# First output stage of a two-layer decoder kernel: the next layer's transposed input is made by VectorE and short-run transfers instead of TensorE

## The chip, the core and the metric

The kernel runs on one core of one Trainium2 chip. The metric is the device time of one execution in microseconds; the time of a kernel is the median of its runs. TensorE is called PE here, VectorE DVE, ScalarE ACT, GpSimd POOL, SyncE SP. "SPq" is SP's queue of transfer issues.

## What is computed

The reference is one inference step of a two-layer decoder trunk on 2048 prompt tokens and 64 sample tokens, width 1024. Each layer projects x, runs two parallel head groups (windowed attention and a gated linear recurrence), and ends in the part that matters here:

```python
mix = jnp.einsum('btc,cd->btd', jnp.concatenate([attn, o_hg], axis=-1), w_out)
h = _layernorm(DN_ALPHA * x + mix, ln_g, ln_b)
gate = jax.nn.sigmoid(jnp.einsum('btd,de->bte', h, w_pg))
y = h + gate * jnp.einsum('btp,pd->btd', p, w_pp)
```

y is the output of the layer and the x of the next one. All is float32; each product is made as three PE products of "high" and "low" parts of its operands.

## The kernel before

The tokens are 17 tiles of 128 (NT = 17; tile 16 holds the samples). Each layer is three stages one after another: attention, recurrence, output. Each stage runs over all 17 tiles. `output_phase` (L1873) is called for layer 0 and for layer 1; `more` is true in layer 0 only, and all that the change touches stands under `more`.

For tile n the output stage does this. PE makes `mix` (L2158), 24 matmuls for each half of 512 columns, into MX. DVE adds the residual row (`add_row`, L2075), normalises (`norm`, L2084), POOL applies gain and bias (`affine`, L1970): the result h lies in `hb[k]`, two buffers by turns. PE transposes h in eight blocks of 128 by 128 into the PSUM tile HT (`turn_h`, L2167). ACT copies HT to `hh` (`high_h`, L2012), DVE makes the remainder `hl` (`low_h`, L2096). PE makes `gate` (L2179, 48 matmuls) out of hh and hl and then `ple` (L2187, 12 matmuls). ACT takes the tanh (L2020); DVE blends and adds into `hb[k]` (`embed`, L2103, two instructions): this is y, and the semaphore `y_done` counts it. SP stores it to `y_all` (`store_y`, L1904).

The next layer reads x with the width on the partitions, from the DRAM tensor `xT1[n]`, shape [128, 8, 128]: partition p, chunk c, token t hold y[t, 128c + p]. Before the change PE makes this: `turn_y(n)` (L2195) transposes the eight blocks of y into HT, once `h_low` shows that DVE has read the h that lay there; ACT copies HT to the SBUF tile `yT` (`copy_yT`, L2022); SP stores `yT` (`store_yT`, L1908), one transfer with 4 KB for each partition.

Each engine has its list of instructions in a fixed order, with semaphores between the engines. The orders around the change:

- PE, step n: mix(n+1) half 0, turn_h(n), mix(n+1) half 1, turn_y(n-1), gate(n), ple(n).
- DVE, step n: low_h(n), add_row(n+1), norm(n+1), embed(n).
- ACT, step n: high_h(n), split_m(n+2), copy_yT(n-1), gate_tanh(n), split_p(n+1).
- SP, step n: load_row(n+2), load_p(n+2), store_y(n), load_m(n+3), store_yT(n-1).

For tile 16 there is no mix left to make. PE runs turn_h(16), turn_y(15), gate(16), ple(16), turn_y(16). SP issues in this stretch store_y(15), store_yT(14), four loads of the next layer's weights (L197), store_yT(15). The y of tile 16 is taken by the next layer directly out of HT.

There is one `yT` tile. Before, ACT waits in copy_yT(n) until the store of tile n-1 has landed (`yT_st`).

Of the kernel before, what the change touches and what calls it, by code (L numbers as in the profile page):

```python
# [25 lines left out]
P = 128  # L26
DEPTH = 2
D = 1024
KC = D // P
# [3 lines left out]
NT = SEQ // P + 1  # L33
# [92 lines left out]
def counted(value, names):  # L126
# [22 lines left out]
    **counted(NT, "m_high m_split mix_ps p_high p_split h_sum stats_done var_done ve_done rstd_done centred scaled h_done hT_ps"),  # L149
    **counted(NT, "h_high h_low gate_ps tanh_done ple_ps blend y_done"),  # L150
    **counted(16 * NT, "m_in row_in p_in"), "ln_in": 32, "y_st0": 16 * (PAIRS + 1), "y_st1": 16 * PAIRS,
    **counted(2 * KC + PC, "w_high w_split"), **counted(NT, "yT_ps yT_sb"), "yT_st": 16 * NT}


class Weights:
# [216 lines left out]
def attention_phase(nc, block, layer, C, dram, S, weights, following, lead, given, prior):  # L372
# [7 lines left out]
    with ExitStack() as ctx:  # L380
# [312 lines left out]
        def _(dve):  # L693
# [110 lines left out]
            if layer == 0:  # L804
                given.prepare(dve)
            else:
                dve.wait_ge(*prior["y_st0"].at(16 * (PAIRS + 1)))
                dve.wait_ge(*prior["y_st1"].at(16 * PAIRS))
                dve.wait_ge(*prior["yT_st"].at(16 * NT))
            dve.tensor_scalar(nsink[:, :], C["sinks"][:, layer, :], -1.0, None, ALU.mult).then_inc(S["sink_done"].sem, 1)  # L810
            dve.wait_ge(*S["sink_done"].at(1))

# [1060 lines left out]
def output_phase(nc, block, layer, C, dram, S, weights, lead, first_part, prior):  # L1873
# [3 lines left out]
    with ExitStack() as ctx:  # L1877
# [12 lines left out]
        @block.sync  # L1890
        def _(sp):
            def load_m(n):
                wait(sp, S["m_split"], n)
                sp.dma_start(mraw[:, :, :], dram["mixT"][tile_of(n)]).then_inc(S["m_in"].sem, 16)

            def load_row(n):
                wait(sp, S["h_sum"], n)
                sp.dma_start(xrow[:, :], dram["x_rows" if layer == 0 else "y_all"][n]).then_inc(S["row_in"].sem, 16)

            def load_p(n):  # L1900
                wait(sp, S["p_split"], n)
                sp.dma_start(praw[:, :, :], dram["pT"][layer, n]).then_inc(S["p_in"].sem, 16)

            def store_y(n, k):  # L1904
                sp.wait_ge(*S["y_done"].at(n + 1))
                sp.dma_start(dram["y_all"][n], hb[k][:, :]).then_inc(stored[k].sem, 16)

            def store_yT(n):  # L1908
                if not more:
                    return  # L1910
                sp.wait_ge(*S["yT_sb"].at(n + 1))
                sp.dma_start(dram["xT1"][n], yT[:, :, :]).then_inc(S["yT_st"].sem, 16)

            load_row(1)
            load_p(1)

            def step(n, k):
                load_row(n + 2)
                load_p(n + 2)
                store_y(n, k)  # L1920
                load_m(n + 3)
                if not (isinstance(n, int) and n == 0):
                    store_yT(n - 1)

            step(0, 0)
            with sp.Fori(1, PAIRS) as j:
                step(2 * j - 1, 1)
                load_row(2 * j + 2)
                load_p(2 * j + 2)
                store_y(2 * j, 0)  # L1930
                with sp.If(j < PAIRS - 1):
                    load_m(2 * j + 3)
                store_yT(2 * j - 1)
            if more:
                sp.wait_ge(*S["mix_ps"].at(NT))
                lead.load(sp, 0, 4)
            store_y(NT - 2, 1)
            store_yT(NT - 3)
            if more:
                lead.load(sp, 4, KC)  # L1940
            store_yT(NT - 2)
            store_y(NT - 1, 0)
            store_yT(NT - 1)
            sp.wait_ge(*S["y_st0"].at(16 * (PAIRS + 1)))
            sp.wait_ge(*S["y_st1"].at(16 * PAIRS))
            if more:
                sp.wait_ge(*S["yT_st"].at(16 * NT))

        @block.gpsimd
        def _(pool):  # L1950
# [49 lines left out]
        @block.scalar  # L2000
        def _(act):
            def split_m(n, k):
                act.wait_ge(*S["m_in"].at(16 * n + 16))
                wait(act, S["mix_ps"], n - 1)
                act.activation(mh[k][:, :, :], mraw[:, :, :], ACT.Copy).then_inc(S["m_high"].sem, 1)

            def split_p(n):
                act.wait_ge(*S["p_in"].at(16 * n + 16))
                wait(act, S["ple_ps"], n)
                act.activation(ph[:, :, :], praw[:, :, :], ACT.Copy).then_inc(S["p_high"].sem, 1)  # L2010

            def high_h(n):  # L2012
                act.wait_ge(*S["hT_ps"].at(n + 1))
                wait(act, S["gate_ps"], n)
                act.activation(hh[:, :, :], HT[:, :], ACT.Copy).then_inc(S["h_high"].sem, 1)

            def gate_tanh(n):
                act.wait_ge(*S["gate_ps"].at(n + 1))
                wait(act, S["y_done"], n)
                act.activation(th[:, :], GT[:, :], ACT.Tanh, scale=0.5).then_inc(S["tanh_done"].sem, 1)  # L2020

            def copy_yT(n):  # L2022
                if not more:
                    return
                act.wait_ge(*S["yT_ps"].at(n + 1))
                wait(act, S["yT_st"], 16 * n)
                act.activation(yT[:, :, :], HT[:, :], ACT.Copy).then_inc(S["yT_sb"].sem, 1)

            split_m(2, 0)
            for c in range(KC, KC + 6):  # L2030
                weights.round(act, S, layer, c)
            high_h(0)
            for c in range(KC + 6, weights.chunks):
                weights.round(act, S, layer, c)

            def step(n, split=None):
                high_h(n)
                if split is not None:
                    split_m(*split)
                if not (isinstance(n, int) and n == 0):  # L2040
                    copy_yT(n - 1)
                gate_tanh(n)
                split_p(n + 1)

            gate_tanh(0)
            split_p(1)
            step(1, (3, 1))
            with act.Fori(1, PAIRS) as j:
                step(2 * j, (2 * j + 2, 0))
                high_h(2 * j + 1)  # L2050
                with act.If(j < PAIRS - 1):
                    split_m(2 * j + 3, 1)
                copy_yT(2 * j)
                gate_tanh(2 * j + 1)
                split_p(2 * j + 2)
            high_h(NT - 1)
            if more:
                act.wait_ge(*S["mix_ps"].at(NT))
                lead.round(act, 0, 4)
            copy_yT(NT - 2)  # L2060
            gate_tanh(NT - 1)
            if more:
                act.wait_ge(*S["ple_ps"].at(NT))
                lead.round(act, 4, 5)
                act.wait_ge(*S["yT_ps"].at(NT))
                lead.split_high(act, HT)
                lead.round(act, 5, 6)
                act.wait_ge(*lead.S["x_split"].at(1))
            copy_yT(NT - 1)
            if more:  # L2070
                lead.round(act, 6, KC)

        @block.vector
        def _(dve):
            def add_row(n, k, mixed=MX):  # L2075
                dve.wait_ge(*S["mix_ps"].at(n + 1))
                dve.wait_ge(*S["row_in"].at(16 * n + 16))
                if more:
                    wait(dve, S["yT_ps"], n - 1)
                wait(dve, stored[k], 16 * (n // 2) if isinstance(n, int) else 8 * (n - k))  # L2080
                dve.scalar_tensor_tensor(out=hb[k][:, :], in0=xrow[:, :], scalar=ALPHA, in1=mixed[:, :],
                                         op0=ALU.mult, op1=ALU.add).then_inc(S["h_sum"].sem, 1)
# [20 lines left out]
            def embed(n, k):  # L2103
# [6 lines left out]
                dve.scalar_tensor_tensor(out=hb[k][:, :], in0=th[:, :], scalar=0.5, in1=hb[k][:, :],  # L2110
                                         op0=ALU.mult, op1=ALU.add).then_inc(S["y_done"].sem, 1)

            add_row(0, 0)
            norm(0, 0)
            add_row(1, 1, HT)
# [6 lines left out]
            def step(n, k):  # L2122
                low_h(n)
                add_row(n + 1, 1 - k)
                norm(n + 1, 1 - k)
                embed(n, k)

            norm(1, 1)
            embed(0, 0)
            step(1, 1)  # L2130
            with dve.Fori(1, PAIRS) as j:
                step(2 * j, 0)
# [11 lines left out]
        def _(pe):  # L2144
# [21 lines left out]

            def turn_h(n, k):  # L2167
                pe.wait_ge(*S["h_done"].at(n + 1))
                if more:
                    wait(pe, S["yT_sb"], n - 1)  # L2170
                else:
                    wait(pe, S["h_low"], n)
                if isinstance(n, int) and n == 0:
                    pe.wait_ge(*S["h_sum"].at(2))
                for c in range(KC):
# [19 lines left out]
            def turn_y(n, k):  # L2195
                if not more:
                    return
                pe.wait_ge(*S["y_done"].at(n + 1))
                pe.wait_ge(*S["h_low"].at(n + 2)) if not (isinstance(n, int) and n == NT - 1) else wait(pe, S["yT_sb"], n)
                for c in range(KC):  # L2200
                    t = pe.transpose(HT[:, c * P:(c + 1) * P], hb[k][:, c * P:(c + 1) * P], C["ident"][:, :])
                t.then_inc(S["yT_ps"].sem, 1)
# [2 lines left out]
            def step(n, k, mixes=True):  # L2205
# [2 lines left out]
                turn_h(n, k)  # L2208
                if mixes:
                    mix(n + 1, 1, 1 - k)  # L2210
                if not (isinstance(n, int) and n == 0):
                    turn_y(n - 1, 1 - k)
                gate(n)
                ple(n)

# [16 lines left out]
                step(2 * j + 1, 1)  # L2232
            n = NT - 1
            turn_h(n, 0)
            turn_y(n - 1, 1)
            gate(n)
            ple(n)
            turn_y(n, 0)
# [225 lines left out]
```

## Time and profile before

| | us |
|---|---|
| median of 3 runs | 2735.33 |
| lowest and highest | 2734.08, 2740.19 |
| the profiled execution, its own time | 2740.13 |
| its span, first to last instruction | 2738.3 |
| PE busy | 2644.4 (97% of the span) |
| DVE busy | 1514.6 (55%) |
| ACT busy | 1048.6 (38%) |
| POOL busy | 1038.6 (38%) |

The profiled execution took 4.80 us more than the median. The output stage of layer 0 lies at about 936 to 1381 us of the span. Times in the rows further on are from the start of the span. A row of the timeline has start, duration, engine, line, operation, written tile, read tiles, and in brackets the idle time before it with what ended it. Matmuls overlap, so that one lasts longer than the distance to the next.

### The profile page before, as it was taken

Reading aid. Unit: us, or ns where it says so; the run is one execution under the profiler, and the core shown is the slowest. Engines: PE = TensorE matmul, PEld = TensorE weight load, DVE = VectorE, ACT = ScalarE, POOL = GpSimd, SP = SyncE. Lnnn points to the kernel's source line nnn. Section 1 sums busy time; section 2 is a strip of 40 time slices with the busy share of each in tenths; the row PEclk is TensorE's granted clock in tenths of the full one; section 3 lists DMA queues with packets and bytes.
Section 4 is the critical chain, followed back from the end, with each engine's and each line's share of the span. In section 5 each row is a group of like instructions: output and inputs, shape, how many; then the busy total and the mean of one; then the engine's idle time right before and its main releaser. Section 6 shows DMA issues by size and latency. Waiting matters only on the chain.

```text
span 2738.3 us, 54412 instructions
## 1 busy us (share of the span) xinstructions
PE 2644.4 (97%) x21010; PEld 2158.7 (79%) x21010; DVE 1514.6 (55%) x3052; ACT 1048.6 (38%) x2305; POOL 1038.6 (38%) x959
## 2 busy tenths in 40 slices
PE   7999989999999799999989999899999997999998
PEld 6777768888888678888777777688888886788887
DVE  5566675777767822222345656657777767322322
ACT  3333354555555511111233333545555555111111
POOL 2222214555555433333212222145555564333232
PEclk9999999999999899999999999989999998999999
DMA  4111141011111522222421111410111005211220
GB/s 169 47 34 46 35 160 47 29 51 40 36 32 38 193 83 77 94 90 73 146 102 47 35 46 36 159 44 33 42 49 36 32 31 200 68 67 66 68 73 33
DMA packets 103450, 190.75 MB, mean 70 GB/s; under 512 B 11744, under 2 KB 64992, under 8 KB 101216
## 3 DMA queue, kind: packets, MB, share of 16 engines
q1 hardware_dynamic: 102864, 188.49, 20.7%
q8 instruction: 112, 1.84, 0.3%
q14 instruction: 42, 0.34, 0.0%
q10 hardware_dynamic: 432, 0.08, 0.0%
HBM read 138.53 MB, written 51.90 MB: 70 GB/s over the span
## 4 chain that ended last, share of the span: by engine, by line
PE 90%; DVE 3%; ACT 2%; issue 2%; DMA 1%; POOL 1%; SPq 1%; DVEq 0%; POOLq 0%; ACTq 0%
PE r_Z L121 25%; PE a_Z L121 16%; PE o_GT L2152 13%; PE o_MX L2152 12%; PE o_PL L2152 3%; PE a_T L977 2%; PE r_LV L1714 2%; PE a_SC L956 2%; PE o_HT L2176 1%; PE r_M L1746 1%; PE r_O L1741 1%; PE r_O L1740 1%; PE a_SC L966 1%; PE r_Z L259 1%; PE r_LV L1710 1%
## 5 line engine op out<-in xcount | busy, mean ns | idle before, releaser
L121 PE MATMUL r_Z<-w_rec_high,w_rec_xh 128*128 128x512 f32 x1024 | 423.4, 414 | 1.5 <-DVE r_kT L1488 0.9
L121 PE MATMUL r_Z<-w_rec_high,w_rec_xl 128*128 128x512 f32 x1024 | 403.7, 394 | 0.0
L121 PE MATMUL r_Z<-w_rec_low,w_rec_xh 128*128 128x512 f32 x1024 | 402.8, 393 | 0.0
L121 PE MATMUL a_Z<-w_attn_high,w_attn_xh 128*128 128x512 f32 (+1 forms) x816 | 304.4, 373 | 15.4 <-DVE w_attn_low L213 13.1
L121 PE MATMUL a_Z<-w_attn_high,w_attn_xl 128*128 128x512 f32 (+1 forms) x816 | 291.7, 357 | 0.0
L121 PE MATMUL a_Z<-w_attn_low,w_attn_xh 128*128 128x512 f32 (+1 forms) x816 | 291.7, 357 | 0.0
L1266 POOL TENSOR_TENSOR r_qE<-r_qT,r_E 128x256 f32<-128x256 f32 x230 | 186.9, 813 | 261.5 <-ACT r_E L1370 150.8
L1370 ACT ACTIVATE r_E<-r_E 128x512 f32<-128x512 f32 x230 | 145.2, 632 | 311.5 <-DVE r_E L1525 309.3
L121 PEld LDWEIGHTS r_Z<-w_rec_high,w_rec_xl 128*128 128x128 f32 x1024 | 193.8, 189 | 42.7
L121 PEld LDWEIGHTS r_Z<-w_rec_high,w_rec_xh 128*128 128x128 f32 x1024 | 193.9, 189 | 41.2 <-issue 2.9
L121 PEld LDWEIGHTS r_Z<-w_rec_low,w_rec_xh 128*128 128x128 f32 x1024 | 194.5, 190 | 34.5
L2152 PE MATMUL o_GT<-w_out_high,o_hh 128*128 128x512 f32 x512 | 203.4, 397 | 5.9 <-issue 5.9
L2107 DVE SCALAR_TENSOR_TENSOR o_th<-o_th,o_PL 128x1024 f32<-128x1024 f32 x34 | 41.5, 1222 | 297.8 <-PE o_PL L2152 297.8
L2152 PE MATMUL o_MX<-w_out_high,o_mh 128*128 128x512 f32 x480 | 191.3, 399 | 11.3 <-POOL o_ml L1954 11.3
L2152 PE MATMUL o_GT<-w_out_low,o_hh 128*128 128x512 f32 x512 | 201.4, 393 | 0.0
L2152 PE MATMUL o_GT<-w_out_high,o_hl 128*128 128x512 f32 x512 | 201.3, 393 | 0.0
L1266 POOL TENSOR_TENSOR r_kE<-r_kT,r_E 128x256 f32<-128x256 f32 x230 | 198.2, 862 | 0.0
L121 PEld LDWEIGHTS a_Z<-w_attn_high,w_attn_xh 128*128 128x128 f32 x816 | 155.7, 191 | 43.7 <-issue 21.4
L2152 PE MATMUL o_MX<-w_out_low,o_mh 128*128 128x512 f32 x480 | 188.4, 392 | 0.0
L2152 PE MATMUL o_MX<-w_out_high,o_ml 128*128 128x512 f32 x480 | 188.3, 392 | 0.0
L2020 ACT ACTIVATE o_th<-o_GT 128x1024 f32<-128x1024 f32 x34 | 35.0, 1029 | 396.9 <-PE o_GT L2152 376.4
L121 PEld LDWEIGHTS a_Z<-w_attn_high,w_attn_xl 128*128 128x128 f32 x816 | 155.6, 191 | 23.9
(290 smaller groups left out, 5633.1 us busy)
## 6 DMA issues: line engine op xcount, KB each, us to landing
dram_y_all<-o_hb SPq DMA_DIRECT2D x34, 512.0 KB, 2.9
w_attn_xraw<-dram_xT SPq DMA_DIRECT2D x33, 512.0 KB, 3.6
w_rec_whole<-dram_w_in SPq DMA_DIRECT2D x16, 1024.0 KB, 13.2
o_mraw<-dram_mixT SPq DMA_DIRECT2D x32, 512.0 KB, 4.3
r_xraw<-dram_xT SPq DMA_DIRECT2D x30, 512.0 KB, 3.6
w_attn_whole<-dram_w_in SPq DMA_DIRECT2D x16, 640.0 KB, 7.7
dram_mixT<-a_mixT SPq DMA_DIRECT2D x136, 64.0 KB, 2.1
dram_mixT<-r_u SPq DMA_DIRECT2D x34, 256.0 KB, 2.2
```

The source lines that it names most:

```text
L121: mm = pe.matmul(out, a[:, c, :], b[:, c, :], start=(first and c == chunks[0] and a is xh and b is wh), stop=(last and c == chunks[-1] and ...
L259: pe.matmul(self.banks[what], x[:, c, :], w.high[:, c, self.columns[what]], start=(c == 0 and x is self.xh[0]), stop=False)
L956: mm = pe.matmul(scores[r:r + 64, 4 * s + i, r:r + 192], qT[rows, i, r:r + 64], keys[:, first_key + r:first_key + r + 192], start=True, st ...
L966: t = pe.transpose(turned[:, h, :], probs[:, h, :], C["ident"][:, :])
L977: mm = pe.matmul(T[d, :], v[tile][:, d], pT[:, i, 4 * s:4 * s + 4, :].rearrange("p h t -> p (h t)"), start=(i == 0), stop=(i == 1))
L1266: op = pool.tensor_tensor(to, halves(flat(q_or_k), h)[half], halves(E[i][:, :], h)[half], ALU.mult)
L1370: act.activation(E[l % 2][:, :], E[l % 2][:, :], ACT.Exp).then_inc(S["level_exp"].sem, 1)
L1710: mm = pe.matmul(to[r:r + NEAR, g * h:g * h + h], kE[i][:, g * P + r:g * P + r + NEAR], qE[i][:, g, q], start=True, stop=True)
L1714: mm = pe.matmul(to[r:r + NEAR, g * 16:g * 16 + 16], kE[i][:, g * P + r:g * P + r + NEAR], qE[i][:, g, r // 2:r // 2 + 16], start=True, st ...
L2020: act.activation(th[:, :], GT[:, :], ACT.Tanh, scale=0.5).then_inc(S["tanh_done"].sem, 1)
L2107: dve.scalar_tensor_tensor(out=th[:, :], in0=th[:, :], scalar=1.0, in1=PL[:, :], op0=ALU.add, op1=ALU.mult).then_inc(S["blend"].sem, 1)
L2152: mm = pe.matmul(out[0][:, out[1]], a[:, c, :], w, start=(c == 0 and a is high and b is wh), stop=(c == chunks - 1 and a is low))
```

## The change

In layer 0, for tiles 0 to 15, PE no longer transposes y and ACT no longer copies it. DVE does it instead: `turn_y(n, k)` stands in DVE's list right behind `embed(n, k)` and turns y within blocks of 32 by 32, straight into `yT`. A block stays at its place, so the four blocks of 32 partitions have to be moved: `store_yT` is now four transfers, one for each group of 32 partitions of `yT`, whose destination is taken apart so that each run is 32 tokens, 128 bytes. `turn_y` waits until the four stores of the tile before have landed. Tile 16 still goes over PE, ACT and one transfer. PE's and DVE's waits on `yT_ps` and `yT_sb` that guarded HT and `hb` are relaxed. The place of `store_yT(n-1)` in SP's list is the same. The core of the diff:

```diff
@@ output_phase, sync engine
                 sp.wait_ge(*S["yT_sb"].at(n + 1))
-                sp.dma_start(dram["xT1"][n], yT[:, :, :]).then_inc(S["yT_st"].sem, 16)
+                if isinstance(n, int) and n == NT - 1:
+                    sp.dma_start(dram["xT1"][n], yT[:, :, :]).then_inc(S["yT_st"].sem, 16)
+                    return
+                to = dram["xT1"][n].rearrange("(q r) c t -> r c q t", q=4)
+                for i in range(0, P, 32):
+                    sp.dma_start(to[:, :, :, i:i + 32], yT[i:i + 32, :, :].rearrange("r c (q t) -> r c q t", q=4))\
+                        .then_inc(S["yT_st"].sem, 16)
@@ scalar engine
             def copy_yT(n):
-                act.wait_ge(*S["yT_ps"].at(n + 1))
-                wait(act, S["yT_st"], 16 * n)
+                act.wait_ge(*S["yT_ps"].at(1))
+                act.wait_ge(*S["yT_st"].at(64 * n))
@@ step, and the same in the loop and for the last tiles
-                if not (isinstance(n, int) and n == 0):
-                    copy_yT(n - 1)
                 gate_tanh(n)
@@ vector engine
                 if more:
-                    wait(dve, S["yT_ps"], n - 1)
+                    wait(dve, S["yT_sb"], n - 1)
...
+            def turn_y(n, k):
+                if not more:
+                    return
+                dve.wait_ge(*S["y_done"].at(n + 1))
+                wait(dve, S["yT_st"], 64 * n)
+                dve.transpose(yT[:, :, :].rearrange("p c t -> p (c t)"), hb[k][:, :]).then_inc(S["yT_sb"].sem, 1)
...
                 embed(n, k)
+                turn_y(n, k)
@@ tensor engine
             def turn_h(n, k):
-                if more:
-                    wait(pe, S["yT_sb"], n - 1)
-                else:
-                    wait(pe, S["h_low"], n)
+                wait(pe, S["h_low"], n)
...
                 if mixes:
                     mix(n + 1, 1, 1 - k)
-                if not (isinstance(n, int) and n == 0):
-                    turn_y(n - 1, 1 - k)
                 gate(n)
                 ple(n)
...
             turn_h(n, 0)
-            turn_y(n - 1, 1)
             gate(n)
```

## Rows read from the trace of the kernel before

**Rows 1.** The page: chain that ended last, shares by engine and by line

```profile
PE 90%; DVE 3%; ACT 2%; issue 2%; DMA 1%; POOL 1%; SPq 1%; DVEq 0%; POOLq 0%; ACTq 0%
```

**Rows 2.** Chain that ended last, 1150 to 1300 us: start, us, work

```profile
1222.77 5.44 PE o_MX L2152 x24
1228.22 0.87 PE o_HT L2176 x8
1229.09 5.46 PE o_MX L2152 x24
1234.55 0.87 PE o_HT L2201 x8
1235.42 10.90 PE o_GT L2152 x48
1246.32 2.72 PE o_PL L2152 x12
```

**Rows 3.** Timeline of DVE, 1196 to 1236 us

```profile
1213.32 0.81 DVE L2093 TENSOR_SCALAR o_hb<-o_hb,o_mv,o_rstd 128x1024 f32<-128x1024 f32 x1 [1.05 <-POOL o_rstd L1968]
...
1224.14 1.23 DVE L2110 SCALAR_TENSOR_TENSOR o_hb<-o_th,o_hb 128x1024 f32<-128x1024 f32 x1
1230.19 1.22 DVE L2099 TENSOR_TENSOR o_hl<-o_HT,o_hh 128x1024 fp32r<-128x1024 f32 x1 [4.82 <-ACT o_hh L2015]
```

**Rows 4.** Timeline of SP's queue, 1170 to 1260 us: start, us, line, transfer

```profile
1226.21 0.33 SPq L1894 DMA_DIRECT2D o_mraw<-dram_mixT  x1
1226.64 0.54 SPq L1912 DMA_DIRECT2D dram_xT<-o_yT  x1
1237.01 0.33 SPq L1898 DMA_DIRECT2D o_xrow<-dram_x_rows  x1
```

**Rows 5.** Transfers issued 1225.4 to 1235 us: count, KB each, us to landing

```profile
dram_xT<-o_yT SPq DMA_DIRECT2D x1, 512.0 KB, 5.4
```

**Rows 6.** Groups of DVE by line: busy, mean ns of one, idle before

```profile
L1550 DVE COPY_PREDICATED r_near<-diagonal,r_M 128x128 f32<-128x128 int32 x34 | 10.4, 306 | 6.0 <-DVE r_near L1542 6.0
```

**Rows 7.** Transfers 1382.2 to 1385.1 us, one store alone: packets; share of 16 engines

```profile
q1 hardware_dynamic: 144, 0.52, 44.7%
...
dram_xT<-o_yT SPq DMA_DIRECT2D x1, 512.0 KB, 2.6
```

**Rows 8.** Transfers 1437 to 1439.5 us, four stores with runs of 512 bytes

```profile
q1 hardware_dynamic: 428, 0.20, 26.9%
```

**Rows 9.** Transfers 1417.6 to 1429.3 us, 16 stores with runs of 256 bytes

```profile
q1 hardware_dynamic: 576, 0.13, 5.1%
```

**Rows 10.** Transfers 24 to 24.5 us, loads with runs of 64 and 128 bytes

```profile
q1 hardware_dynamic: 907, 0.09, 144.9%
```

**Rows 11.** Transfers 1386.4 to 1386.9 us, the start of a load of 1024 runs

```profile
q1 hardware_dynamic: 184, 0.09, 69.5%
```

**Rows 12.** Chain that ended last, 1355 to 1375 us: the last tile

```profile
1357.85 0.14 issue
...
1359.05 12.51 PE o_GT L2152 x48
```

**Rows 13.** Stages: us, busy of PE, PEld, DVE, ACT, POOL, then granted clock, DMA share

```profile
1354.98:1357.98 3.00, 0.01 (x1) 0.03 (x1) 2.96 (x4) 2.96 (x3) 0.45 (x1) 1.00 0.14 57
1359.40:1362.80 3.40, 3.40 (x10) 2.62 (x9) 3.40 (x3) 2.30 (x3) 0.00 (x0) 0.50 1.01 295
...
1401.00:1402.00 1.00, 1.00 (x11) 1.00 (x10) 0.00 (x0) 0.54 (x3) 0.00 (x0) 1.00 0.28 109
```

**Rows 14.** Who waited for whom, PE, 1396 to 1402 us

```profile
PE a_SC L929 <- POOL a_qk L518: 1.9, 1, 1.9
```

**Rows 15.** Chain that ended last, 955 to 1060 us: the first tiles

```profile
970.00 1.70 PE o_HT L2201 x8
```

**Rows 16.** Timeline of SP's queue, 1350 to 1364 us

```profile
1356.73 0.35 SPq L1906 DMA_DIRECT2D dram_y_all<-o_hb  x1
```

**Rows 17.** Timeline of ACT, 1340 to 1470 us

```profile
1374.31 1.27 ACT L203 ACTIVATE w_attn_high<-w_attn_whole 128x1280 fp32r<-128x1280 f32 x1 [1.69 <-PE o_PL L2152]
```

More of the change, by code:

```diff
@@ L151 @@
     **counted(16 * NT, "m_in row_in p_in"), "ln_in": 32, "y_st0": 16 * (PAIRS + 1), "y_st1": 16 * PAIRS,
-    **counted(2 * KC + PC, "w_high w_split"), **counted(NT, "yT_ps yT_sb"), "yT_st": 16 * NT}
+    **counted(2 * KC + PC, "w_high w_split"), "yT_ps": 1, "yT_sb": NT, "yT_st": 64 * NT - 48}
 class Weights:
@@ L808, in _ @@
                 dve.wait_ge(*prior["y_st1"].at(16 * PAIRS))
-                dve.wait_ge(*prior["yT_st"].at(16 * NT))
+                dve.wait_ge(*prior["yT_st"].at(64 * NT - 48))
             dve.tensor_scalar(nsink[:, :], C["sinks"][:, layer, :], -1.0, None, ALU.mult).then_inc(S["sink_done"].sem, 1)
@@ L1946, in _ @@
             if more:
-                sp.wait_ge(*S["yT_st"].at(16 * NT))
+                sp.wait_ge(*S["yT_st"].at(64 * NT - 48))
         @block.gpsimd
@@ L2052, in _ @@
                     split_m(2 * j + 3, 1)
-                copy_yT(2 * j)
                 gate_tanh(2 * j + 1)
@@ L2059, in _ @@
                 lead.round(act, 0, 4)
-            copy_yT(NT - 2)
             gate_tanh(NT - 1)
@@ L2064, in _ @@
                 lead.round(act, 4, 5)
-                act.wait_ge(*S["yT_ps"].at(NT))
+                act.wait_ge(*S["yT_ps"].at(1))
                 lead.split_high(act, HT)
@@ L2126, in step @@
                 embed(n, k)
+                turn_y(n, k)
             norm(1, 1)
             embed(0, 0)
+            turn_y(0, 0)
             step(1, 1)
@@ L2198, in turn_y @@
                 pe.wait_ge(*S["y_done"].at(n + 1))
-                pe.wait_ge(*S["h_low"].at(n + 2)) if not (isinstance(n, int) and n == NT - 1) else wait(pe, S["yT_sb"], n)
+                pe.wait_ge(*S["h_low"].at(n + 1))
                 for c in range(KC):
```

## The prediction

> **What bounds the kernel now.** I read the page first, to see what the end waits for: PE holds 90% of the chain that ended last [rows 1]. Then the chain in order of time inside the output stage of layer 0: one tile is 5.44 + 0.87 + 5.46 + 0.87 + 10.90 + 2.72 = 26.27 us, from 1222.77 to 1249.04, and every piece is PE [rows 2]. So PE's list alone sets the pace here, and turn_y is 0.87 us of it, on the path. Then the timelines of DVE and of SP's queue, for when y is done and when its stores go out. DVE ends y at 1224.14 + 1.23 = 1225.37 and stands idle 4.82 us, until low_h at 1230.19 [rows 3]. SP then issues three transfers in a row: the y store, the load of mixT, the yT store at 1226.64 [rows 4]; the last lands 5.4 us later, at 1232.04 [rows 5]. Before the change that landing matters to nobody for most of a tile. The change makes DVE wait for it.
>
> **The new order, which decides.** In DVE's list turn_y(n) comes right after embed(n), and it waits until the stores of tile n-1 have landed, since there is one yT tile. But SP issues the stores of tile n-1 only behind store_y(n), which itself waits for y of tile n. yT(n-1) has lain ready for a whole tile, and its stores still start after y(n) is done. So the time from issue to landing stands in the open between embed(n) and turn_y(n), once for each tile. Queued behind turn_y(n) on DVE is low_h(n+1), and gate(n+1) on PE waits for that.
>
> **Part by part.**
>
> Removed from PE: 8 transposes a tile, 0.87 us on the path [rows 2]. ACT's copy and its wait cost nothing today and give nothing: ACT's work lies beside PE's. The relaxed waits (HT, hb) are met long before and are worth nothing.
>
> Added to DVE: one transpose of 128 by 1024. The trace has none. From both sides: 0.81 us, what DVE needs for a one-source instruction of that size [rows 3]; 2.45 us, if it costs as much as eight instructions of 128 by 128 at 306 ns [rows 6]. I take 1.22, as the other instructions of 1024 columns.
>
> The four stores: 4 x 32 x 32 = 4096 runs of 128 bytes instead of 128 runs of 4 KB. What one 4 KB-run store costs the 16 engines: 44.7% of 2.9 us = 1.30 us [rows 7]. Price of a short packet, as engine time over packets: at 512 bytes 0.269 x 2.5 x 16 / 428 = 25 ns [rows 8]; at 256 bytes, a store to DRAM as here, 0.051 x 11.7 x 16 / 576 = 16.6 ns [rows 9]; at 64 and 128 bytes, loads, 1.449 x 0.5 x 16 / 907 = 12.8 ns [rows 10]. The trace has no store with runs of 128 bytes; the nearest row is the 256-byte store, and I take its price: 4096 x 16.6 / 16 = 4.25 us, bounds 3.28 (12.8 ns) and 6.43 us (25 ns). Against the transfer engines stands the rate at which packets are fed: at the start of a load of 1024 runs, 184 packets went in 0.5 us with the engines at 69.5% [rows 11], 2.7 ns a packet, which would make 11.1 us of 4096. Upper bound.
>
> The Trainium skill has a rule against this change: page "DMA: Bandwidth & Descriptors", Specifications, says that under 512 bytes a transfer misses line rate because of read-modify-write. The rows at 256 and 64 bytes show packets getting cheaper with size, though not in proportion, and no jump. The same page, "Why small descriptors are slow (HBM only)", has a fixed overhead of about 3 cycles per packet, 11 cycles at 256 bytes; that would be 7 at 128, so by an estimate from it 16.6 x 7/11 = 10.6 ns, 2.7 us a tile, and a time of about 2749 by the same sum as below, between the cheap end and rival B.
>
> Now one middle tile, in the times of the tile from 1222.77. Landing of the stores: 1232.04 - 1.30 + 4.25 = 1234.99. The four issues, 0.54 us each as today, end by 1228.8, while the engines are still busy with y and mixT, and SP's next issue is at 1237.01 [rows 4]: cost nothing. Turn: +1.22 = 1236.21; low_h behind it +0.04 +1.22 = 1237.47; gate 0.14 later [rows 12] = 1237.61. Without the stall gate would start at 1234.55, where turn_y stands today. PE is idle 3.06 us, and gate starts 1237.61 - 1235.42 = 2.19 us later than before.
>
> **The clock.** After an idle time of PE of 3.00 us the granted clock fell from 1.00 to 0.50, so from 2.4 to 1.2 GHz [rows 13], and the gate behind it took 12.51 us instead of 10.90 [rows 2, 12]: 1.61 us. After an idle time of 1.9 us [rows 14] it stayed 1.00 [rows 13]. My 3.06 us is on the side where it falls, just. So a middle tile is 2.19 + 1.61 = 3.80 us longer.
>
> Tiles with this wait: turn_y(1) to turn_y(14), in front of gates 2 to 15: 14 x 3.80 = 53.2 us.
>
> First: turn_y(0) waits for no store. It puts 1.26 us in front of low_h(1) and takes PE's transposes, 1.70 us at the low clock [rows 15], out: -0.4 us.
>
> Last: turn_y(15) waits for the stores of tile 14, which SP issues behind the y store of 1356.73 [rows 16]. There is no mix to cover anything. The y store lands in 2.6 us [rows 7], 1359.33; +4.25 +1.22 +0.04 +1.22 +0.14 = 1366.20 for gate(16), against 1359.05 [rows 12]: +7.1 us. The low clock is there already today. The four weight loads that SP issues behind these stores come some 3 us later; ACT first needs one of them at 1374.31 [rows 17], so nothing.
>
> Tile 16 is as before. Sum: 53.2 - 0.4 + 7.1 = 59.9 us on the profiled execution's 2740.13, 2800.0; that execution is 4.80 above the median of 2735.33, so 2795 beside the median.
>
> **Rivals.**
>
> Cheap end of the same mechanism: 12.8 ns and a turn of 0.81 us. Gate starts at 1230.74 (today's landing less today's moving) + 3.28 + 0.81 + 1.40 = 1236.23; PE idle 1.7 us, clock stays up; 14 x 0.81 = 11.3, last tile +5.8, first -0.8: +16, 2751. This belongs to the forecast's case and is its lower end.
>
> A. Packets or their feed are dear: 25 ns and a turn of 2.45 us give 14 x (5.6 + 1.6) + 10.6 + 0.8 = +112, 2847; the feed of 2.7 ns a packet lands the stores 11.1 us and what a store takes beside its moving, 2.6 - 1.3 us [rows 7], behind the first issue, at 1239.0: 14 x (6.2 + 1.6) + 13.1 - 0.4 = +122, 2857. For it: the start of that load [rows 11]. Against: 907 short packets moved within 0.5 us elsewhere [rows 10], though those may have been fed earlier. 0.25. The read-modify-write rule of the page named above would put the time here.
>
> B. Not slower: a packet costs in proportion to its bytes, half of 16.6 ns. The stores then take 2.12 us, gate starts at 1235.48, +0.04 a tile: what turn_y gave is just eaten; 14 x 0.04 + 5.0 - 0.4 = +5, 2740.5. It decides from about 8.3 ns a packet down. Against it: from 512 to 256 bytes the price fell by a third only, and at 64 bytes it is still 12.8 ns [rows 8 to 10]. 0.08.
>
> C. All hidden: the stores cost no more than 1.2 us, under 5 ns a packet; then 14 x -0.87 + 4.1 - 0.4 = -8.5, 2727. Nothing in the rows goes so low. 0.03.
>
> D. The stores don't move runs of 128 bytes but single elements. At 12.8 ns, 131072 of them take 105 us a tile; some 1,400 us longer. The last dimension is contiguous on both sides, so 0.01.
>
> **How the numbers follow.** The forecast, an open stall between 1.7 and 4 us with or without the clock, has 0.60, rival A 0.25, B 0.08, C 0.03, D 0.01, and 0.03 stays for something worse than A. The range reaches from below the cheap end, 2745, to the top of A, 2860, and leaves out B, C, D and the rest, some 0.15. A measurement of this kernel can tell about 0.2% (5.5 us) from no change. Faster by more: C and a little of B, 0.04. Within: B and the cheapest end, 0.07. Slower: 0.89.
>
> **What the profile after would show.** The chain of the stage no longer PE alone: in each tile PE waits in front of gate for DVE's low_h, some 3 us, about 14 times; DVE waits in front of its transpose for the landing of the xT stores; 4096 more packets a tile under 512 bytes; granted clock at 0.5 for a few us of each tile; tiles of about 30.0 us where they were 26.27. The transpose between 0.8 and 2.5 us. Gate in the last tile near 1366 on the old scale. I am wrong if the tile is shorter than 26.27 us, or if DVE's wait ends before low_h would be due; then the price of a 128-byte packet is the step that failed. If tiles are 28.4 us and the clock stays up, only the clock term was wrong.

## The result, and the profile after

| | before | after |
|---|---|---|
| median of the five runs side by side, us | 2737.48 | 2759.71 |
| lowest and highest, us | 2734.08, 2741.49 | 2757.54, 2765.86 |
| the profiled execution, its own time and span, us | 2740.13, 2738.3 | 2759.71, 2757.9 |

The changed kernel is slower: 1.0081 times the time, interval 1.0067 to 1.0095, some 22 us. The forecast was 2795, 60 us more than before. The side and the mechanism are as forecast, the size is little more than a third of it.

The page of the changed kernel has these lines: busy time of each engine, the DMA packets, and the chain that ended last, by engine.

```profile
PE 2634.0 (96%) x20882; PEld 2144.3 (78%) x20882; DVE 1531.6 (56%) x3068; ACT 1032.0 (37%) x2289; POOL 1038.2 (38%) x959
...
DMA packets 167707, 190.76 MB, mean 69 GB/s; under 512 B 78048, under 2 KB 131296, under 8 KB 165472
...
PE 86%; DVE 4%; issue 3%; ACT 2%; DMA 2%; SPq 2%; POOL 1%; DVEq 0%; POOLq 0%; ACTq 0%
```

PE has 10.4 us less work than before (2644.4) and the kernel is 20 us longer. PE's share of the chain went from 90% [rows 1] to 86%, DMA and SP's queue from 1% each to 2% each. The bytes are the same; the packets under 512 bytes, 11744 before, are 66,304 more: 4096 for each of 16 tiles, and 768, which is 16 for each of the 48 added stores (one store alone had 128 + 16 packets [rows 7]).

The chain of one tile in order of time, from the gate of one tile to the gate of the next (start, us, what). It answers to [rows 2].

```profile
1217.89 11.17 PE o_GT L2163 x48
1229.06 2.73 PE o_PL L2163 x12
...
1233.14 1.24 DVE o_hb L2112
...
1235.65 0.62 SPq L1917
...
1237.47 1.71 SPq L1917
...
1239.37 2.96 DMA dram_xT<-o_yT
...
1243.52 1.20 DVE o_hl L2101
...
1244.95 11.17 PE o_GT L2163 x48
```

Before, every piece of this chain was PE. Now it leaves PE at the end of `ple` (1231.78), goes over `embed` on DVE (y is done at 1234.38), the issues of the four stores on SP, their landing at 1242.33, and over `low_h` back to `gate` at 1244.95. From gate to gate it is 27.06 us in this tile, where it was 26.27. DVE's timeline shows the transpose, PE's the first matmul of gate with the idle time before it, and SP's queue the issues; they answer to [rows 3, 4].

```profile
1242.35 1.25 DVE L2120 STREAM_TRANSPOSE o_yT<-o_hb 128x1024 f32<-128x1024 f32 x1 [7.98 <-DMA dram_xT<-o_yT]
```
```profile
1244.95 0.49 PE L2163 MATMUL o_GT<-w_out_high,o_hh 128*128 128x512 f32 x1 [1.40 <-DVE o_hl L2101]
```
```profile
1235.22 0.34 SPq L1894 DMA_DIRECT2D o_mraw<-dram_mixT  x1
1235.65 4.32 SPq L1917 DMA_DIRECT2D dram_xT<-o_yT  x4
```

DVE stood idle for 7.98 us in front of its transpose, waiting for the stores of the tile before; low_h stands behind it (1243.52 in the chain); PE was idle for 1.40 us. Over the whole stage the list of waits (engine and tile, released by; us in total, times, longest) has

```profile
DVE o_yT L2120 <- DMA dram_xT<-o_yT: 118.6, 15, 8.8
...
PE o_GT L2163 <- DVE o_hl L2101: 20.9, 13, 2.2
```

and the chain has the gates of tiles 2 and 14 and of the last two:

```profile
998.39 12.78 PE o_GT L2163 x48
...
1326.90 12.75 PE o_GT L2163 x48
...
1354.14 10.88 PE o_GT L2163 x48
...
1369.69 9.16 issue
1378.85 12.65 PE o_GT L2163 x48
```

Eleven of the 13 gates behind a stall took 11.16 to 11.19 us, those of 998.39 and 1326.90 took 12.78 and 12.75. In the last tile PE is idle for 10.23 us in one piece, of which 9.16 us follow ACT's copy in the chain; the kernel before had 3.00 us there. The "issue" in this row is a wait of which the chain doesn't find the end: DVE's rows have the transpose of tile 15 at 1376.39, behind a wait of 6.06 us for the landing, and then low_h of tile 16.

**Where the time went.** From the start of ple(0) to the high part of tile 16 on ACT (`w_attn_xh`), the two chains are 415.51 us (963.41 to 1378.92) and 436.56 us (961.43 to 1397.99): 21.05 us more. The whole spans of the two profiled executions differ by 19.6 us, so the change's cost lies in this stretch. Its parts:

- ple(0) to gate(1): 8.29 before, 7.81 after, -0.48. gate(1), at the low clock in both: 11.89 and 12.68, +0.79.
- End of gate(1) to start of gate(15): 356.90 and 372.23 us, +15.33. That is the 13 idle times, 20.9; less 14 times turn_y of 0.87, -12.2; the 11 gates of 11.17 instead of 10.90, +3.0; the two at 12.77, +3.7. Together 15.4.
- Start of gate(15) to start of gate(16): 18.56 and 24.71, +6.15.
- Behind it: -0.7.

### The profile page after: what moved, and what is told of

The parts are those of the page before. It is cut to its first block, busy times and chain, and to the rows that moved or that the text cites. A ratio compares the mean times of both kernels' runs of the same rounds, so it can differ in the third digit from the quotient of the medians.

```text
span 2757.9 us, 54273 instructions
## 1 busy us (share of the span) xinstructions
PE 2634.0 (96%) x20882; PEld 2144.3 (78%) x20882; DVE 1531.6 (56%) x3068; ACT 1032.0 (37%) x2289; POOL 1038.2 (38%) x959
## 4 chain that ended last, share of the span: by engine, by line
PE 86%; DVE 4%; issue 3%; ACT 2%; DMA 2%; SPq 2%; POOL 1%; DVEq 0%; POOLq 0%; ACTq 0%
PE r_Z L121 24%; PE a_Z L121 16%; PE o_GT L2163 13%; PE o_MX L2163 10%; PE o_PL L2163 3%; PE a_T L977 2%; PE r_LV L1714 2%; PE a_SC L956 2%; PE a_SC L966 1%; PE r_M L1746 1%; PE r_O L1741 1%; PE r_O L1740 1%; PE o_HT L2184 1%; PE r_Z L259 1%; PE r_LV L1710 1%
## 5 line engine op out<-in xcount | busy, mean ns | idle before, releaser
L2163 PE MATMUL o_GT<-w_out_high,o_hh 128*128 128x512 f32 x512 | 205.3, 401 | 41.2 <-DVE o_hl L2101 20.9
```

What stands on the lines that cost most here:

```text
L2163: mm = pe.matmul(out[0][:, out[1]], a[:, c, :], w, start=(c == 0 and a is high and b is wh), stop=(c == chunks - 1 and a is low))
```

## The experiments

**The theory** was that the order decides: SP issues the stores of tile n-1 only behind y of tile n, DVE waits for their landing with low_h queued behind, so the landing stands in the open. **The rival** was that the short runs cost by themselves, through the engines they load, wherever they stand. Four kernels tell these apart. Ratios are against the kernel before, run beside each.

**The stores one step earlier.** SP issues the stores of tile n in step n, right behind `load_m(n+3)`, and doesn't wait for the next tile.

```diff
                 load_m(n + 3)
-                if not (isinstance(n, int) and n == 0):
-                    store_yT(n - 1)
+                store_yT(n)
...
-                store_yT(2 * j - 1)
+                store_yT(2 * j)
...
             store_y(NT - 2, 1)
-            store_yT(NT - 3)
```

> The changed kernel, but SP issues the four stores of tile n behind store_y(n) and load_m(n+3), a tile earlier, so that they land while PE works on the next tile. Theory 1 (the order): the loss is the landing that stands between embed and low_h; it is gone, PE's tile is 26.27 - 0.87 = 25.40 us, 14 x -0.87 = -12, the first gate -0.4, the last +0.3: about 2725, DVE waits for no landing. Rival (the stores themselves: 4096 short packets, SP's longer issues, DRAM traffic cost the time wherever they stand): stays near 2760.

Measured: 2729.80 us, ratio 0.9963 (0.9951 to 0.9976). Same 4096 runs for each tile, same four issues, and it is faster than the kernel before. The chain of a tile in this kernel is PE alone:

```profile
1202.34 10.88 PE o_GT L2161 x48
1213.22 2.72 PE o_PL L2161 x12
1215.94 5.44 PE o_MX L2161 x24
1221.38 0.87 PE o_HT L2182 x8
1222.25 5.46 PE o_MX L2161 x24
1227.71 10.88 PE o_GT L2161 x48
```

It is [rows 2] without the 0.87 of turn_y: 25.37 us, every gate 10.88. So the change's gain is real, 0.9 us a tile, and what the changed kernel lost was the place of the stores. In the last tile PE is still idle for 4.30 us in front of gate(16), 2.95 us in the next kernel.

**The transpose behind low_h.** The stores stay where the change has them; DVE turns y one step later, with low_h ahead of it.

```diff
                 low_h(n)
+                turn_y(n - 1, 1 - k)
                 add_row(n + 1, 1 - k)
                 norm(n + 1, 1 - k)
                 embed(n, k)
-                turn_y(n, k)
```

(with the same move ahead of the loop, and turn_y of tile 15 behind low_h of tile 16)

> The changed kernel with SP's order as it is, but on DVE turn_y(n) stands behind low_h(n+1) instead of in front of it. The wait for the landing is kept; only what is queued behind it changes. Theory 1: DVE still waits some us for the landing, but gate(n+1) on PE has its h_low by then: 14 x -0.87, the first gate about -1.5, gate(16) -1.1: about 2723. Rival (the stores themselves): near 2760.

Measured: 2726.13 us, ratio 0.9951 (0.9936 to 0.9965). DVE's timeline in this kernel:

```profile
1223.96 1.23 DVE L2101 TENSOR_TENSOR o_hl<-o_HT,o_hh 128x1024 fp32r<-128x1024 f32 x1 [4.83 <-ACT o_hh L2021]
1227.27 1.25 DVE L2120 STREAM_TRANSPOSE o_yT<-o_hb 128x1024 f32<-128x1024 f32 x1 [2.08 <-DMA dram_xT<-o_yT]
```

DVE still waits for the landing, 2.08 us here and 35.0 us over the stage, and it costs nothing, since behind the transpose there is now add_row, which PE doesn't need for most of a tile. The landing was not made faster; only what is queued behind the wait was changed.

**Both.**

> Both changes of order together. Theory 1: no more to gain than by either, about 2722 to 2724, and DVE's wait for the landing is gone as well. Were the two parts of the loss separate ones (stores and turn each with its own), it would be clearly under either alone.

Measured: 2725.21 us, ratio 0.9953 (0.9938 to 0.9968), the same as the second alone; of the versions here these two are the best. In this kernel the four stores go out into an idle queue, and SP's row is

```profile
1223.13 2.98 SPq L1917 DMA_DIRECT2D dram_xT<-o_yT  x4
```

instead of 4.32 us behind y and mixT.

**The kernel before, with short runs.** PE and ACT turn y as before; only the store is cut into four of 32 tokens each, which makes the same 4096 runs of 128 bytes.

```diff
-                sp.dma_start(dram["xT1"][n], yT[:, :, :]).then_inc(S["yT_st"].sem, 16)
+                for i in range(0, P, 32):
+                    sp.dma_start(dram["xT1"][n][:, :, i:i + 32], yT[:, :, i:i + 32]).then_inc(S["yT_st"].sem, 16)
```

> The kernel before (TensorE turns y, ScalarE copies it), with its one store of yT cut into four of 32 tokens: 4 x 1024 runs of 128 bytes, as many short packets and issues as in the changed kernel. ScalarE's copy of the next tile waits for them, a tile later. Theory 1 (short runs cost nothing with a tile of cover): within 0.2% of before, 2737; tile 26.27 us; at the last tile ScalarE's copy may wait longer. Rival (short packets disturb the other transfers or SP): slower by some us, loads of mixT and rows land later and PE waits.

Measured: 2740.04 us beside 2738.61, ratio 1.0013 (1.0002 to 1.0023). Its chain still has 26.26 us from gate to gate:

```profile
1206.77 10.89 PE o_GT L2153 x48
...
1233.03 7.04 PE o_GT L2153 x31
```

SP's issues of a tile are 4.25 us here too. Where the landing has cover, the short runs cost at most 0.2%. The rival falls.

**The size.** What is left is why the landing came earlier than forecast and why the forecast put more on the clock than the chip did. Five kernels vary the stores in the changed kernel's order.

**Long runs.** The same four stores of 32 partitions, each with runs of 4 KB; the placing is left out, so xT1 holds the blocks where they lie.

```diff
-                    sp.dma_start(to[:, :, :, i:i + 32], yT[i:i + 32, :, :].rearrange("r c (q t) -> r c q t", q=4))\
+                    sp.dma_start(dram["xT1"][n][i:i + 32, :, :], yT[i:i + 32, :, :])\
```

> The changed kernel with the four stores as they are in number and order, but each writes its 32 partitions with one run of 4 KB, 32 packets instead of 1024. It leaves the placing out, so xT1 holds y in the wrong order. Price of a packet as cause of the remaining stall: from the landing 10.5 us behind the last ple, 2.6 us of moving become 1.3, landing at 9.2, PE's stall 0.2 instead of 1.7 us: 13 x -1.4 and the last tile -1.3, about 2738 to 2740. Rival (SP's four issues, 4.3 us in the trace of after, set the landing): unchanged issues, near 2758.

Measured: 2737.14 us, ratio 0.9996 (0.9984 to 1.0009). The stalls are nearly gone; the list of waits and DVE's timeline have

```profile
PE o_GT L2163 <- DVE o_hl L2101: 2.9, 6, 1.2
```
```profile
1209.06 1.25 DVE L2120 STREAM_TRANSPOSE o_yT<-o_hb 128x1024 f32<-128x1024 f32 x1 [6.70 <-DMA dram_xT<-o_yT]
```

DVE's wait is 6.70 us instead of 7.98: the short runs are worth 1.3 us of landing, and PE's idle time in front of the middle gates goes with it, from 20.9 us over the stage to 2.9. No middle gate has the low clock either, and the kernel is 22.6 us faster than the changed one. With long runs the last tile still has PE idle for 8.93 us, which eats what the middle tiles gain. This run alone doesn't part packets from issues: the rival had taken SP's issues to be unchanged, and the four took 2.07 us here instead of 4.32.

**Two queues.** Two of the four stores are issued by ACT in tiles 0 to 14, under the same conditions, to halve SP's time of issuing.

```diff
+            def store_half(n):
+                act.wait_ge(*S["y_done"].at(n + 1))
+                act.wait_ge(*S["yT_sb"].at(n))
+                to = dram["xT1"][n - 1].rearrange("(q r) c t -> r c q t", q=4)
+                for i in (64, 96):
+                    act.dma_start(to[:, :, :, i:i + 32], yT[i:i + 32, :, :].rearrange("r c (q t) -> r c q t", q=4))\
+                        .then_inc(S["yT_st"].sem, 16)
```

> The changed kernel with the issues of the four stores shared: two by SP as before, two by ScalarE, which waits for y_done(n) like SP and stands idle there. Same packets, same moment. If in the changed kernel SP's issues (four at 0.78 us, the third held 1.7 us) set the landing: last issue some 2 us earlier, landing at 8.5 to 9.5 us behind the last ple instead of 10.5, PE's stall under 0.5: 2738 to 2745. If the packets in the 16 engines do (10 ns each behind y and mixT): landing unchanged, 2756 to 2762.

Measured: 2760.17 us, ratio 1.0092 (1.0073 to 1.0111), the changed kernel's time. SP's queue, ACT's and DVE's rows:

```profile
1212.90 2.63 SPq L1917 DMA_DIRECT2D dram_xT<-o_yT  x2
```
```profile
1211.75 1.71 ACTq L2035 DMA_DIRECT2D dram_xT<-o_yT  x2
```
```profile
1219.88 1.25 DVE L2132 STREAM_TRANSPOSE o_yT<-o_hb 128x1024 f32<-128x1024 f32 x1 [8.29 <-DMA dram_xT<-o_yT]
```

SP is done 2.63 us behind its first store where it was 4.32, ACT's two run beside it, and DVE's wait is no shorter, 8.29 us and 7.98 before. So in the changed kernel the work queued for the transfer engines (y, mixT and the short runs) sets the landing; SP's third issue of 1.71 us is SP being held, not the cause. One thing besides was changed: ACT's two stores start at 1211.75, ahead of the load of mixT at 1212.37. The landing counts the last of them all, and it isn't earlier for that.

This kernel also shows something on the clock. PE was idle for 1.59 to 2.47 us in front of 13 gates, and not one of them had the low clock, all took 11.17 to 11.19 us. The longest of these idle times, in PE's timeline:

```profile
1031.25 0.49 PE L2175 MATMUL o_GT<-w_out_high,o_hh 128*128 128x512 f32 x1 [2.47 <-DVE o_hl L2113]
```

**Eight issues.** The same 4096 runs, in eight stores of 16 partitions.

```diff
                 for i in range(0, P, 32):
+                    for r in (0, 16):
+                        sp.dma_start(to[r:r + 16, :, :, i:i + 32],
+                                     yT[i + r:i + r + 16, :, :].rearrange("r c (q t) -> r c q t", q=4))\
+                            .then_inc(S["yT_st"].sem, 16)
```

> The changed kernel with eight stores of 16 partitions each: the same 4096 runs of 128 bytes, twice the issues on SP and twice the completion packets. If packets set the landing: within 0.3 us a tile, 2760 to 2766. If SP's issues (0.6 to 0.75 us each) set it: four more are 2.4 to 3 us a tile, some 2800 to 2820 with the clock.

Measured: 2799.22 us, ratio 1.0218 (1.0200 to 1.0237). The side that expected a cost of issuing (2800 to 2820) was right and the one by packets (2760 to 2766) wrong. SP's row and the end of the chain of a tile:

```profile
1200.90 6.11 SPq L1918 DMA_DIRECT2D dram_xT<-o_yT  x8
```
```profile
1235.68 0.60 SPq L1918
...
1236.46 2.67 DMA dram_xT<-o_yT
...
1241.75 12.77 PE o_GT L2165 x48
```

An issue comes every 0.78 us (0.60 and the register work around it), eight take 6.1 us, and the last store lands 2.67 us behind the start of its issue, as long as the one store of 512 KB took alone (2.6 [rows 7]). Behind the end of y the landing is at 9.48 us. By an estimate from this, with issues alone to wait for, four stores would land at 9.48 - 4 x 0.78 = 6.4 us; it is 7.95 in the changed kernel. So with four the packets set the landing, 1.6 us later than issues alone would, and with eight the issues do. This kernel also has PE idle for 2.9 us in front of nearly every gate, which is what the forecast had for the changed kernel, and it costs 39.5 us more than that one.

**Runs of 64 bytes.** Eight stores with 1024 runs of 16 tokens each, 8192 packets.

```diff
+                    for t in (0, 16):
+                        sp.dma_start(to[:, :, :, i + t:i + t + 16],
+                                     yT[i:i + 32, :, :].rearrange("r c (q t) -> r c q t", q=4)[:, :, :, t:t + 16])\
+                            .then_inc(S["yT_st"].sem, 16)
```

> The changed kernel with runs of 64 bytes: eight stores of 1024 packets. If a packet costs about the same whatever its size down here (10 ns, as 4096 packets in 2.6 us say), moving takes 2.6 us longer, PE's stall grows from 1.7 to 4.3 us, and behind a stall of that length the clock falls to 0.5 and costs 1.6 us more: 13 x 4.2 + 2.6 = +57, about 2817. If the price goes with the bytes: near 2760 to 2765. If the clock term is wrong and only the moving counts: about 2796.

Measured: 2832.20 us, ratio 1.0344 (1.0328 to 1.0360), above what was expected. SP's row:

```profile
1219.45 7.30 SPq L1918 DMA_DIRECT2D dram_xT<-o_yT  x8
```

Beside the eight issues of 128-byte runs the landing is 1.4 us later (10.85 us behind y against 9.48), SP's issues end 1.2 us later, and PE is idle 4.3 to 4.7 us in front of 13 gates, which all take 12.5 us or more. Issues and packets can't be told apart in this one, so it gives no price of a 64-byte packet, only an upper bound: 2903 packets went in the 2.0 us from 1223, 11.0 ns each in an engine. So the forecast for this run, a stall and the low clock in front of 13 gates, came true, and the size was 15 us short.

**The stores ahead of mixT.** SP issues the four stores behind the y store and only then the load of mixT.

```diff
                 store_y(n, k)
-                load_m(n + 3)
                 if not (isinstance(n, int) and n == 0):
                     store_yT(n - 1)
+                load_m(n + 3)
```

> The changed kernel, but SP issues the four stores ahead of load_m(n+3) instead of behind it, still behind store_y(n). What is queued ahead in the transfer engines is then 1.3 us less: landing 1.3 us earlier, PE's stall from 1.7 to about 0.4 us: 13 x -1.3 = -17, about 2743. The load lands later, but it has most of a tile. If the queue ahead does not count: 2760.

Measured: 2734.62 us, ratio 0.9984 (0.9973 to 0.9995). SP's queue, DVE and the gates of the chain:

```profile
1224.35 3.13 SPq L1917 DMA_DIRECT2D dram_xT<-o_yT  x4
1227.80 0.40 SPq L1894 DMA_DIRECT2D o_mraw<-dram_mixT  x1
```
```profile
1229.85 1.25 DVE L2120 STREAM_TRANSPOSE o_yT<-o_hb 128x1024 f32<-128x1024 f32 x1 [6.12 <-DMA dram_xT<-o_yT]
```
```profile
1207.54 10.88 PE o_GT L2163 x48
...
1232.91 10.88 PE o_GT L2163 x48
```

The landing comes 8.7 us behind ple instead of 10.55. It is enough: PE doesn't wait, the tile is 25.37 us, the middle of the stage is that of the two best versions. That this kernel is still 8 us slower than the second experiment is the last tile, where there is no mixT to go past: PE is idle for 10.23 us there, as in the changed kernel. The chains of this kernel and, under it, of the second experiment, where ACT has copied h of tile 16 and PE stands in front of gate(16):

```profile
1348.92 1.03 ACT o_hh L2021
1349.95 9.16 issue
```
```profile
1344.33 1.03 ACT o_hh L2021
1345.36 1.88 issue
```

9.16 against 1.88 us is 7.3 us, and gate(16) behind it took 13.66 us against 12.77.

## Why the prediction came out as it did

**The mechanism: right.** The chain runs as forecast, from ple over embed, the stores of the tile before, the transpose and low_h to gate, and in the middle tiles it can be switched off by the order on DVE, by the order on SP, or by a landing 1.9 us earlier. The rivals with packets or their feed so dear that a tile is 6 us longer, and those in which nothing stands open, are out.

**Durations named one by one.** The transpose is 1.25 us, 1.22 was taken. From landing to gate it is 1244.95 - 1242.33 = 2.62 us, the sum of the forecast, partly by luck: gate starts 0.23 us behind low_h where 0.14 was taken, and low_h starts 0.08 us before the transpose has ended. The first tile is -0.48 (-0.4). The last is +6.15 (+7.1).

**The step that failed first: the price of a 128-byte packet.** The landing was put 12.22 us behind the end of ple (1234.99 for a tile from 1222.77) and is 10.55 us behind it (1242.33 for 1231.78). By the forecast's own sum: from the end of y to the landing it was 6.67 us with one store and is 7.95 with four, so moving takes 1.30 + 1.28 = 2.58 us, 10.1 ns a packet, where 16.6 was taken from [rows 9] and 12.8 [rows 10] was the lower bound. (The 1.30 us are share times time as well; but the packets of that store all lie within some 1.4 us of its window, so they are at most 0.1 us short.) Two windows of half a microsecond, one behind the other while the stores of this tile move, show it directly (queue, packets, MB, share):

```profile
q1 hardware_dynamic: 854, 0.11, 138.1%
```
```profile
q1 hardware_dynamic: 818, 0.10, 131.5%
```

1672 packets in 1.0 us over 16 engines are 9.6 ns each. By the share it would be 13 ns, and a share of 138% can't be time of 16 engines: packets overlap inside an engine, and the share adds up the duration of each. So share times time over packets, as the forecast worked it out, is no price. [rows 10] said so before the change, with its 144.9%: 907 packets in 0.5 us are 8.8 ns by count over time, and I divided the share by them. [rows 9] is a window with the engines mostly idle (5.1%): what is read there is how long one packet takes, and nothing in it says how many an engine handles in a time. The upper bound by feeding, 2.7 ns a packet from [rows 11], falls with the same windows: 1672 packets in 1.0 us are one every 0.6 ns.

The estimate from the Trainium skill in the prediction, 10.6 ns (page "DMA: Bandwidth & Descriptors", section "Why small descriptors are slow (HBM only)"), lies beside the 9.6 and 10.1 ns of this trace, and the time it gave, 2749, is off by 11 us where the forecast is off by 35. That is luck in part: all that was taken from the page is the ratio 7 to 11, and it was put on the 16.6 ns of [rows 9], the reading that failed.

The short runs did move at half the pace of the long ones: 512 KB took 2.58 us in runs of 128 bytes and 1.30 us in runs of 4 KB. The rule of the Trainium skill (page "DMA: Bandwidth & Descriptors", section Specifications), that a transfer under 512 bytes misses line rate because of a read-modify-write, fits this in its first half. No run here shows whether a read-modify-write is the reason, and the price is far from the 25 ns of rival A.

With the right price alone the forecast's sum would have been too low: 14 x (3.06 - 1.67 - 0.87) = 7.3, the last tile +5.5, the first -0.4, together +12 us where the two chains differ by 21. What is missing then is in the next two steps and in small parts of the outer tiles.

**The second: the clock term.** The forecast had PE idle for 3.06 us and the clock fall in front of each of 14 gates, 22.5 us. With the landing earlier, PE is idle for 1.35 to 2.21 us, and the granted clock fell behind two of the 13. Windows of the changed kernel on two gates (us, busy of PE, PEld, DVE, ACT, POOL, then granted clock, DMA share, GB/s):

```profile
998.50:1009.00 10.50, 10.50 (x40) 8.47 (x41) 3.08 (x5) 0.00 (x0) 5.52 (x4) 0.84 0.17 50
...
1245.00:1256.00 11.00, 11.00 (x49) 9.10 (x50) 3.15 (x5) 0.00 (x0) 5.52 (x4) 1.00 0.17 48
```

In the first, part of the gate ran at 1.2 GHz instead of 2.4 (mean 0.84); in the second the clock was 1.00 throughout. The sum of the forecast's middle tiles was 14 x (3.06 - 0.87 + 1.61) = 53.2 against 15.4 measured, 37.8 too much: 42.8 - 20.9 = 21.9 of it is idle time, and 22.5 - 6.7 = 15.8 is what the gates lose. The price of a fallen clock was nearly right (12.77 against 10.90, 1.9 us, where 1.61 was taken). How often it falls followed in the main from the wrong landing. The kernel with eight issues has the idle time that the forecast had, and there it falls in front of 10 of 14 gates, not of all. The forecast also let the length of the idle time alone decide, and that doesn't hold: it fell behind 1.95 us in the changed kernel and not behind 2.47 us in the one with two queues.

**A step left out: the gate behind a short stall.** Eleven gates took 11.17 us (the clock of the one above was 1.00), 0.27 more than 10.90, 3.0 us together. PE's rows of gate(15), which had no stall, show where it lies:

```profile
1353.75 0.39 PE L2163 MATMUL o_MX<-w_out_high,o_ml 128*128 128x512 f32 x1
1353.98 0.39 PE L2163 MATMUL o_GT<-w_out_high,o_hh 128*128 128x512 f32 x1
```

Without a stall the first matmul of gate starts 0.16 us before the last one of mix has ended (1354.14), and the chain counts the gate from there; behind an idle time this overlap is lost. And the first matmul behind a stall takes 0.49 us instead of 0.39, with the next one 0.33 us behind it instead of 0.22. A long stall isn't needed: in the kernel with long runs a gate behind an idle time of 0.21 us took 11.19 us. Why the first matmul takes longer stays open.

**A count: 13 tiles, not 14.** In front of gate(15) there is no stall. There the condition in SP's loop leaves out the load of mixT, so the stores aren't behind it; the kernel with the stores ahead of mixT shows that this alone is enough.

**"The issues cost nothing": right for four, for another reason than given.** They were put at 0.54 us each. They take 0.60 and come every 0.78 us, 3.0 us for four into an idle queue, 4.3 behind y and mixT. In the changed kernel they don't set the landing, as the two queues show, but with eight they do; the room was 1.6 us, two issues.

## What to carry to other kernels

When work moves from a busy engine to an idle one, look first at what stands in the idle engine's list behind the new instruction: here the same transpose with the same stores is 0.8% slower ahead of `low_h` and 0.5% faster behind it. A store out of a single buffer belongs where its data are ready, not behind the next tile's result, and it belongs ahead of loads that nobody waits for soon. Price short packets by count over time in a stretch where the engines are full; the share of a queue adds up overlapping packets and overstates it.

## What the runs showed of the hardware

- Packets of 128 bytes from SBUF to DRAM took 9.6 to 10.1 ns each in an engine with the queue full, some 2.6 us for 4096 of them over 16 engines, where the same bytes in packets of 4 KB took 1.3 us. In the kernel with both moves, where nothing is ahead of them, it is 2711 in 2.0 us, 11.8 ns, at the pace of an issue of 1024 packets every 0.78 us.
- A transpose of 128 by 1024 float32 within blocks of 32 by 32 took DVE 1.25 us, as much as its other instructions of 1024 columns.
- An issue of 1024 short runs took SP 0.60 us and 0.18 of register work around it; behind y and mixT the third was held for 1.71 us.
- The granted clock isn't settled by the length of the idle time alone. In the changed kernel it fell behind idle times of 1.98 and 1.95 us and not behind one of 2.21; in the kernel with two queues it fell behind none of 13, the longest 2.47 us. In the kernel with eight issues, the idle times in front of its gates are 2.4 to 3.8 us; behind 2.92 us it fell in some tiles and not in others, and of its 14 gates four were fast, those of 1094.21, 1183.15, 1271.94 and 1360.72, every third one. With the runs of 64 bytes it fell in all 13 tiles with 4.3 us or more, where gates took 12.5 to 14.0 us, and not in the one with 2.60. What else decides stays open.
